# A decoder trunk on one core: router by token tile, top-2 by comparing all pairs, and the setup of the experts in another order

## The reference, cut to what matters

```python
def moe_swiglu(x, router, w13, w2):
    logits = (x @ router).astype(jnp.float32)             # 256 x 8
    top_vals, top_idx = lax.top_k(logits, TOP_K)          # TOP_K = 2
    top_w = jax.nn.softmax(top_vals, axis=-1)
    gates = jnp.einsum('bsk,bske->bse', top_w, jax.nn.one_hot(top_idx, N_EXPERTS, dtype=jnp.float32))
    out = jnp.zeros_like(x)
    for e in range(N_EXPERTS):                            # 8 experts, width 3584
        out = out + gates[..., e:e + 1].astype(x.dtype) * swiglu(x, w13[e], w2[e])
    return out
```

## Time and profile before

| | us |
|---|---|
| median of 3 runs | 1828.35 |
| lowest, highest | 1824.98, 1829.74 |
| the profiled execution | 1832.96 |
| its span, first to last instruction | 1831.1 |
| mean granted clock of TensorE, share of full | 0.98 |
| busy: PE, DVE, ACT | 1743.0 (95%), 1291.2 (71%), 983.5 (54%) |

### The profile page before, as it was taken

The page is one execution under the profiler, slowest core; times in us unless marked ns, Lnnn a source line. Parts: engine busy times, 40 slices in busy tenths (PEclk is TensorE's granted clock), DMA queues, the critical chain, the costliest instruction groups (busy, mean ns, idle before and its releaser), DMA issues.

```text
span 1831.1 us, 21349 instructions
## 1 busy us (share of the span) xinstructions
PE 1743.0 (95%) x7850; PEld 1354.0 (74%) x7850; DVE 1291.2 (71%) x1209; ACT 983.5 (54%) x871; POOL 22.1 (1%) x32
## 2 busy tenths in 40 slices
PE   7989998998989999879999999999999999999996
PEld 6846565887777465657888888888888888888884
DVE  4465525554454655248989889899899898898996
ACT  4353222434333422117767777677777776777772
POOL 0001000000000010000000000000000000000000
PEclk9999999999999999979999999999999999999998
DMA  8512432645634233278999999999999999999991
GB/s 290 183 63 83 154 116 96 225 150 177 217 138 146 93 115 108 76 253 297 358 344 368 371 346 362 353 358 366 338 363 370 347 359 359 349 369 343 364 369 43
DMA packets 206470, 465.94 MB, mean 254 GB/s; under 512 B 11952, under 2 KB 14544, under 8 KB 206416
## 3 DMA queue, kind: packets, MB, share of 16 engines
q1 hardware_dynamic: 200880, 463.76, 70.4%
q10 hardware_dynamic: 5536, 1.45, 0.3%
HBM read 464.13 MB, written 1.05 MB: 254 GB/s over the span
## 4 chain that ended last, share of the span: by engine, by line
PE 90%; DVE 5%; ACT 2%; DMA 1%; issue 1%; ACTq 0%; DVEq 0%; SPq 0%
PE ps L1483 22%; PE ps L1927 16%; PE ps L1929 16%; PE ps L1928 16%; PE ps L1513 5%; PE ps L1849 3%; PE ps L1907 2%; PE ps L1916 1%; DVE w_lo L903 1%; PE ps L1444 1%; PE ps L1639 1%; PE ps L1775 1%; PE ps L1757 1%; PE ps L1694 1%; PE ps L1596 1%
## 5 line engine op out<-in xcount | busy, mean ns | idle before, releaser
L903 DVE TENSOR_TENSOR w_lo<-ring,w_hi 128x2048 fp32r<-128x2048 f32 x336 | 768.0, 2290 | 120.4 <-ACT w_hi L586 117.6
L586 ACT CAST w_hi<-ring 128x2048 fp32r<-128x2048 f32 x336 | 642.0, 1911 | 279.9 <-PE ps L1929 265.0
L1927 PE MATMUL ps<-w_hi,xe_hi 128*128 128x512 f32 x896 | 353.2, 394 | 3.2 <-DVE w_lo L903 1.8
L1929 PE MATMUL ps<-w_hi,xe_lo 128*128 128x512 f32 x896 | 349.3, 390 | 0.0
L1928 PE MATMUL ps<-w_lo,xe_hi 128*128 128x512 f32 x896 | 348.7, 389 | 0.0
L1927 PEld LDWEIGHTS ps<-w_hi,xe_hi 128*128 128x128 f32 x896 | 168.3, 188 | 38.7 <-DVE w_lo L903 2.8
L1929 PEld LDWEIGHTS ps<-w_hi,xe_lo 128*128 128x128 f32 x896 | 168.2, 188 | 35.7
L1928 PEld LDWEIGHTS ps<-w_lo,xe_hi 128*128 128x128 f32 x896 | 168.4, 188 | 33.8
L1927 PE MATMUL ps<-w_hi,he_hi 128*128 128x512 f32 x448 | 178.2, 398 | 0.0
L1929 PE MATMUL ps<-w_hi,he_lo 128*128 128x512 f32 x448 | 174.8, 390 | 0.0
L1928 PE MATMUL ps<-w_lo,he_hi 128*128 128x512 f32 x448 | 174.4, 389 | 0.0
(11 more groups left out here) (264 smaller groups left out, 1778.4 us busy)
## 6 DMA issues: line engine op xcount, KB each, us to landing
ring<-in_moe_w_dram SPq DMA_DIRECT2D x336, 1024.0 KB, 5.2
ring<-in_ffd_w_dram SPq DMA_DIRECT2D x31, 1024.0 KB, 5.1
ring<-in_w_in_dram SPq DMA_DIRECT2D x24, 1024.0 KB, 5.2
ring<-in_xa_wkv_dram SPq DMA_DIRECT2D x16, 1024.0 KB, 5.0
ring<-in_w_out_dram SPq DMA_DIRECT2D x8, 1024.0 KB, 5.0
ring<-in_xa_wq_dram SPq DMA_DIRECT2D x8, 1024.0 KB, 5.0
ring<-in_xa_wo_dram SPq DMA_DIRECT2D x8, 1024.0 KB, 5.0
ring<-in_ffd_w_dram SPq DMA_DIRECT2D x4, 512.0 KB, 3.5
```

The source lines that it names most:

```text
L586: act.copy(w_hi[:, q % SPLIT_SLOTS, :], ring[:, q % RAW_SLOTS, :]).then_inc(hi_ready, 1)
L903: dve.tensor_tensor(w_lo[:, q % SPLIT_SLOTS, :], ring[:, q % RAW_SLOTS, :], w_hi[:, q % SPLIT_SLOTS, :].bitcast(F32), ALU.subtract).then_i ...
L1927: pe.matmul(ps[:, bank, :], x_hi, hi[:, c, cols], start=first, stop=False)
L1929: return pe.matmul(ps[:, bank, :], x_lo, hi[:, c, cols], start=False, stop=last)
```

## The change

- TensorE turns tile 0 of the last `x2` between the two output panels of tile 1, multiplies tile 0's router products behind the second panel, and tile 1's behind its own transposes. ACT copies tile 0's blocks ahead of its first three casts. VectorE copies tile 0's blocks ahead of the first residual, moves low half 0 between the two residuals, and low half 1 between the last layer norm and the copy of tile 1.
- The two largest are found by comparing all pairs: `order` of an expert is the number of experts that stand above it (a greater logit, or an equal one of a lower index), and `chosen` is `order < 2`. The one-hot rows `oh` and the two logits come after `chosen_ready`.
- `slot` is (rank + 1) * chosen, one step, and is compared with a row 1..128 (`place`).
- The two count products go behind the gathers, into bank 4, with a semaphore of their own; the accumulator's setup goes behind the second `xe_lo`.
- `item(0)` waits for the first half of the gather before its first weight half and for the second before its second.

```diff
--- before.py
+++ after.py
@@ -108,10 +108,11 @@
         lower = (i // half) % 2 == 0
         level[:, v, :] = (block[:, None] == block[~lower][None, :]) & lower[:, None]
     square = np.stack([np.eye(P), i[:, None] < i[None, :], np.ones((P, P)),
-                       np.broadcast_to(i[None, :], (P, P))], 1).astype(np.float32)
+                       np.broadcast_to(i[None, :] + 1, (P, P))], 1).astype(np.float32)
     freq = (THETA ** (-np.arange(0, 2 * ROPE, 2, dtype=np.float32) / np.float32(2 * ROPE))).astype(np.float32)
     e = np.arange(NE, dtype=np.float32)
-    rows = np.concatenate([freq, NE - e, e, np.arange(EXTRA, dtype=np.float32)])
+    earlier = (e[None, :] < e[:, None]).astype(np.float32).ravel()
+    rows = np.concatenate([freq, e, earlier])
     rows = np.broadcast_to(rows[None, :], (P, rows.size)).astype(np.float32)
     return {"mask_a": mask_a, "mask_b": mask_b, "level": level, "square": square,
             "rows": np.ascontiguousarray(rows)}
@@ -136,11 +137,11 @@
         x = sb("x", [P, T, D])
         ln_gb = sb("ln_gb", [P, 2, D])
         square = sb("square", [P, 4, P])
-        ident, before, ones, iota = (square[:, n, :] for n in range(4))
-        rows = sb("rows", [P, ROPE + 2 * NE + EXTRA])
+        ident, before, ones, place = (square[:, n, :] for n in range(4))
+        rows = sb("rows", [P, ROPE + NE + NE * NE])
         freq = rows[:, 0:ROPE]
-        desc = rows[:, ROPE:ROPE + NE]
-        eid = rows[:, ROPE + NE:ROPE + 2 * NE]
+        eid = rows[:, ROPE:ROPE + NE]
+        earlier = rows[:, ROPE + NE:].rearrange("p (e f) -> p e f", e=NE)
         w_router = sb("w_router", [P, KC, NE])
         stats = sb("stats", [P, T, 2, 6])
         mv = sb("mv", [P, T, 2])
@@ -149,6 +150,8 @@
         mhalf = sb("mhalf", [P, 8])
 
         lg = sb("lg", [P, 2, T, NE])
+        above = sb("above", [P, 2, T, NE, NE])
+        order = sb("order", [P, T, NE])
         oh = sb("oh", [P, 2, T, NE])
         rtmp = sb("rtmp", [P, T, NE])
         rmx = sb("rmx", [P, 4, T])
@@ -299,7 +302,8 @@
         hT_psum = [sem(f"hT_psum{t}") for t in range(T)]
         hT_sb = [sem(f"hT_sb{t}") for t in range(T)]
         w2_ready = sem("w2_ready")
-        logit_psum, chosen_ready, rank2_psum = sem("logit_psum"), sem("chosen_ready"), sem("rank2_psum")
+        logit_psum, chosen_ready = sem("logit_psum"), sem("chosen_ready")
+        rank2_psum, count_psum = sem("rank2_psum"), sem("count_psum")
         gate_diff, gate_exp = sem("gate_diff"), sem("gate_exp")
         table_ready = sem("table_ready")
         raw_in = [sem(f"raw_in{s}") for s in range(RAW_SLOTS)]
@@ -727,10 +731,11 @@
                     turn_split(TURN["x2", l], (0,))
                     split_high(2)
                 else:
+                    turn(TURN["x2", l], xT, (0,))
                     act.wait_ge(xo_ready, T * (l + 1))
                     for q in range(SPLIT_SLOTS):
                         high(q, 0, first=True)
-                    turn(TURN["x2", l], xT)
+                    turn(TURN["x2", l], xT, (1,))
                 if l == 0:
                     for n in range(FFN_CHUNKS + 1):
                         if n < FFN_CHUNKS:
@@ -1224,10 +1229,12 @@
                 if l == 0:
                     split_low(1)
                 else:
-                    low(0, 0)
+                    turn(TURN["x2", l], xT, (0,))
                 residual(l, o_p, 0, 1)
                 if l == 0:
                     split_low(1)
+                else:
+                    low(0, 0)
                 residual(l, o_p, 1, 1)
                 if l == 0:
                     turn_split(TURN["x2", l], (0,))
@@ -1235,8 +1242,8 @@
                     layer_norm(3 * l + 1, x, 1)
                     turn_split(TURN["x2", l], (1,))
                 else:
-                    turn(TURN["x2", l], xT, (0,))
                     layer_norm(3 * l + 1, x, 1)
+                    low(1, 0)
                     turn(TURN["x2", l], xT, (1,))
                 if l == 0:
                     for n in range(FFN_CHUNKS + 1):
@@ -1280,45 +1287,43 @@
                     turn_split(TURN["x3", l], (0,))
                     split_low(3)
 
-            low(1, 0)
             low(2, 0)
 
-            dve.wait_ge(logit_psum, 1)
-            dve.tensor_scalar(acc, x[:, :, :], ALPHA, None, ALU.mult).then_inc(acc_init, 1)
             full = [P, T, NE]
 
             def over(v):
                 return v.unsqueeze(2).to_broadcast(full)
 
+            pairs = [P, T, NE, NE]
+            dve.wait_ge(logit_psum, T)
             done(dve.tensor_copy(lg[:, 0], ps[:, 4, 0:T * NE].rearrange("p (t e) -> p t e", t=T)))
+            done(dve.tensor_tensor(above[:, 0], lg[:, 0].unsqueeze(2).to_broadcast(pairs),
+                                   lg[:, 0].unsqueeze(3).to_broadcast(pairs), ALU.subtract))
+            done(dve.scalar_tensor_tensor(above[:, 1], above[:, 0], 0.0, earlier.unsqueeze(1).to_broadcast(pairs),
+                                          ALU.is_equal, ALU.mult))
+            done(dve.scalar_tensor_tensor(above[:, 0], above[:, 0], 0.0, above[:, 1], ALU.is_gt, ALU.add))
+            done(dve.tensor_reduce(order[:, :, :], above[:, 0], AX, ALU.add))
+            done(dve.tensor_scalar(chosen[:, :, :], order[:, :, :], 2.0, None, ALU.is_lt))
+            dve.sem_inc(chosen_ready, 1)
+            dve.memset(slot[:, :, :], -1.0)
             for c in range(2):
-                done(dve.tensor_reduce(rmx[:, c, :], lg[:, c], AX, ALU.max))
-                done(dve.tensor_tensor(rtmp[:, :, :], lg[:, c], over(rmx[:, c, :]), ALU.is_equal))
-                done(dve.tensor_tensor(rtmp[:, :, :], rtmp[:, :, :], desc.unsqueeze(1).to_broadcast(full), ALU.mult))
-                done(dve.tensor_reduce(rmx[:, 3, :], rtmp[:, :, :], AX, ALU.max))
-                done(dve.tensor_tensor(oh[:, c], rtmp[:, :, :], over(rmx[:, 3, :]), ALU.is_equal))
-                if c == 0:
-                    done(dve.tensor_scalar(rtmp[:, :, :], oh[:, 0], -3e38, None, ALU.mult))
-                    done(dve.tensor_tensor(lg[:, 1], rtmp[:, :, :], lg[:, 0], ALU.add))
-            done(dve.tensor_tensor(chosen[:, :, :], oh[:, 0], oh[:, 1], ALU.add))
-            dve.sem_inc(chosen_ready, 1)
-            done(dve.memset(slot[:, :, :], -1.0))
-
-            dve.wait_ge(rank2_psum, 1)
-            done(dve.tensor_tensor(rtmp[:, :, :], ps[:, 5, 0:T * NE].rearrange("p (t e) -> p t e", t=T), chosen[:, :, :],
-                                   ALU.mult))
-            done(dve.tensor_scalar(lg[:, 0], chosen[:, :, :], -1.0, 1000.0, ALU.add, ALU.mult))
-            done(dve.tensor_tensor(slot[:, :, 0:NE], rtmp[:, :, :], lg[:, 0], ALU.add))
-
-            def select(i):
-
-                for t in range(T):
-                    ins = dve.tensor_scalar(sel[:, t, :], iota, slot[:, t, bass.ds(i, 1)], None, ALU.is_equal)
-                ins.then_inc(sel_ready, 1)
-
-
+                done(dve.tensor_scalar(oh[:, c], order[:, :, :], float(c), None, ALU.is_equal))
+                done(dve.tensor_tensor(lg[:, 1], oh[:, c], lg[:, 0], ALU.mult))
+                done(dve.tensor_reduce(rmx[:, c, :], lg[:, 1], AX, ALU.add))
             done(dve.tensor_tensor(rmx[:, 2, :], rmx[:, 1, :], rmx[:, 0, :], ALU.subtract))
             dve.sem_inc(gate_diff, 1)
+
+            dve.wait_ge(rank2_psum, 1)
+            done(dve.scalar_tensor_tensor(slot[:, :, 0:NE], ps[:, 5, 0:T * NE].rearrange("p (t e) -> p t e", t=T), 1.0,
+                                          chosen[:, :, :], ALU.add, ALU.mult))
+
+            def select(i):
+
+                for t in range(T):
+                    ins = dve.tensor_scalar(sel[:, t, :], place, slot[:, t, bass.ds(i, 1)], None, ALU.is_equal)
+                ins.then_inc(sel_ready, 1)
+
+
             select(0)
             dve.sem_inc(he_ready, 1)
             dve.sem_inc(y_split, 2)
@@ -1335,6 +1340,7 @@
 
             for g in range(2):
                 gather_low(0, -2, g, g + 1)
+            dve.tensor_scalar(acc, x[:, :, :], ALPHA, None, ALU.mult).then_inc(acc_init, 1)
             dve.wait_ge(gate_exp, 1)
             done(dve.tensor_scalar(rmx[:, 3, :], rmx[:, 2, :], 1.0, None, ALU.add))
             done(dve.reciprocal(rmx[:, 0, :], rmx[:, 3, :]))
@@ -1349,7 +1355,8 @@
 
                 if part == 0:
 
-                    done(dve.tensor_scalar(cnt[:, 0, :], ps[:, 5, 32:32 + NE], float(P), None, ALU.is_gt))
+                    dve.wait_ge(count_psum, 1)
+                    done(dve.tensor_scalar(cnt[:, 0, :], ps[:, 4, 32:32 + NE], float(P), None, ALU.is_gt))
                     done(dve.tensor_tensor_scan(cnt[:, 1, :], ones[:, 0:NE], cnt[:, 0, :], 0.0, ALU.mult, ALU.add))
                     done(dve.tensor_scalar(table[:, 0:1], cnt[:, 1, NE - 1:NE], float(NE), None, ALU.add))
                     done(dve.tensor_tensor(cnt[:, 2, :], cnt[:, 1, :], cnt[:, 0, :], ALU.subtract))
@@ -1405,7 +1412,7 @@
                     if q == 20:
                         select(i + 1)
```

(39 more changed lines are left out.)

4 lines of the change are left out of this document (2 added, 2 removed).

## The result

The changed kernel takes 1817.58 us (1813.92 to 1820.27, 6 runs) against 1829.61 us (1824.98 to 1834.03, 6 runs) for the kernel before: ratio 0.9937, 95% interval 0.9919 to 0.9954. Its profiled execution has a span of 1816.1 us and a mean granted clock of 0.988.

The account below looks back on a forecast made before the run. Matmuls pace the experts, so the turn-taking chain before the first expert matmul counts: 3.6 + 1.1 + 1.2 + 0.9 + 0.6 + 1.0 = 8.4 us off the median 1828.35 gives 1820.0 us, range 1815.5 to 1824.6.

Parts of the forecast that it names:

- router of tile 0 into the gap: Before tile 1's transposes: tile 0's router products run in TensorE's 5.39 us idle gap, so logits come 3.6 us earlier.
- accumulator off the path: In front of the logits' copy on VectorE: moving the accumulator's setup behind the second xe_lo saves 1.1 us.
- choice by pairs, to the end of chosen: From logits' copy to chosen: 14 instructions in 2.87 us become a sum of 1.66, saving 1.2 us.
- ranks, to the slots' step: From chosen to the next VectorE step: five rank products become three, 2.52 us becomes 1.65, saving 0.9 us.
- slots, to the gathers: Between the ranks and the gathers: one fused step is left of the first four, saving 0.6 us.
- gathers' end to first expert product: TensorE waits for the first xe_lo alone, count products go in the gap: 1.0 us saved, 0.6 at the other bound.
- The bound: Experts are paced by matmuls, so an earlier first expert matmul, 822.04 us now, is worth its whole lead to the end.
- The pair instructions: In the choice of experts: four instructions on 128 elements take 1.28 to 1.54 us with gaps; 1.28 was taken.
- A: Tile 0's router products hold the clock up before tile 1's transposes: 1.4 us more gain, 1818.6 us; chance 0.12.
- B: Clock comes back later, with gathers, counts and first 12 expert matmuls low: gain 4.7 us, 1823.6 us; chance 0.14.
- C: Experts begin at the low clock and stay there: 1835 us with the first six halves low; chance 0.05.
- D: Tile 0's router misses the gap because its xT copy is late: 3.5 us come back, 1823.4 us; chance 0.05.

Follow-up runs that it names:

- order_undone: Changed kernel with the router's order as before: both tiles turned behind the second panel, router products together, low halves put back; 1825.32 us, ratio 0.998.
- lows_later: Changed kernel with low half 1 behind the copy of tile 1's xT and low half 2 behind the selection; 1820.63 us, one execution.
- pairs_undone: Changed kernel with the two experts chosen by maximum, comparison, tie-break and masking as before; 1813.94 us, one execution.
- both_banks: Changed kernel with the wait for both halves of the gather before the first expert product; 1821.05 us, one execution.
- narrow_fit: Changed kernel with TensorE's gaps filled by 14, 8, 8 and 4 idle products of 8 columns; ratio to before 0.9968.
- warm_lows_values: Changed kernel with low halves 1 and 2 later, 3, 0, 2 and 0 idle products, logit values and ACT's exponential behind the gathers; ratio to before 0.9932.
- The second measurement: The changed kernel measured once more without edit; 1820.94 us against 1829.52 for the kernel before, ratio 0.9959.
- warm_fit: Changed kernel with 3.5, 2, 2 and 1 idle products of 512 columns cut to TensorE's gaps; ratio to before 0.9942.
- warm: Changed kernel with six, three, three and two idle 128x512 products in TensorE's gaps; ratio to before 0.9949.
- warm_fit_values: Changed kernel with 3.5, 2, 2 and 0 idle products of 512 columns, logit values and ACT's exponential behind the gathers; ratio to before 0.9937.

## Why the prediction was right, step by step

The forecast was 8.4 us off the median; the stretch gave 9.63, of which 0.89 is the clock in the gathers, which the prediction named as a spread and didn't price in the sum. The steps, each as the lead gained at it from the traces set together at the panel's start:

```
step                                    predicted   measured   from
router of tile 0 into the gap           3.6         3.66       806.42 - 776.37 against 797.52 - 771.13
accumulator off the path                1.1         1.14       807.56 - 806.42
choice by pairs, to the end of chosen   1.2         1.19       2.87 against 1.68
ranks, to the slots' step               0.9         0.78       2.52 against 1.74
slots, to the gathers                   0.6         0.73       1.48 against 0.75
gathers                                 0           0.89       6.17 against 5.28
gathers' end to first expert product    1.0         1.24       1.44 against 0.20
sum                                     8.4         9.63
```

- **The bound** was read rightly: from the first expert product to the end all profiles have between 1007.98 and 1009.14 us, whatever came before.
- **The router.** Its part is right, and order_undone shows it with the low halves' places (3.70). Inside it two small terms were off. Tile 1's transposes come 0.51 us earlier against the panel and not 0.16: the eight between the panels cost 0.87 us (778.08 to 778.95) and not 1.04, and TensorE answers the norm (790.74) in 0.11 us where it took 0.31, for which no run here shows a cause. When the router starts, 0.25 of the 0.51 is left: the transposes were 0.16 shorter (1.78 against 1.94), but they end at 792.63, low half 1 holds VectorE and the copy starts at 793.10, 0.47 later where it had been 0.04. So the half was not quite hidden, as the prediction had it; lows_later takes 0.41 of the router's wait away.
- **The pair instructions** took 0.29 us each, at the lower of the two bounds; a broadcast operand on both inputs (the row at 797.73) took as long as none (798.38). pairs_undone has 1.03 for it, which is the 1.19 less 0.14 that the values cost behind the new choice.
- **Ranks.** Here the cover was thin, and the prediction's 1.57 us of values against 1.65 of products came out the other way: the difference ends at 800.63 + 0.16 = 800.79, the ranks at 800.18 + 0.57 = 800.75, and the row of the slots' step at 800.94 shows no wait for TensorE. In pairs_undone, without those values, the same step comes 0.14 us sooner behind `chosen` and does wait for TensorE. That is the missing 0.1.
- **Half a gather** is worth 1.24 and not 1.0. The prediction put the count products at 0.43 us behind the gathers; from their start to the first expert product they took 0.36 (806.81 to 807.17), and they start 0.16 before the gathers' end as the profile has it, so 0.20 is left. both_banks shows the wait at 1.25.
- **Rivals.** A, that the router's narrow products hold the clock up: the granted clock was 0.55 on the mean from 790 to 800 us in the changed kernel, and in narrow_fit it fell behind nothing but such products. The Trainium skill, "TensorE: Matmul & The Clock Gate", section "What's actually happening", has the clock follow how busy the engine has been. The trace does not agree with that if busy is what the profile counts: narrow_fit fell at 100% busy. B and C, the clock coming back later: where it had fallen it was back before the gathers ended in all profiles. Counted from the gathers' start it came back sooner than in the kernel before in the changed kernel's two profiles (gathers 5.28 and 5.29) and later in lows_later and warm_lows_values (6.57 and 6.61, against 6.17), and never as late as the experts. D: the router of tile 0 did run in the gap. No run showed the slower side.

The mechanism is right up to the gathers: 7.4 us were forecast there and 7.50 measured. The good fit of the time is in part luck. The median of 1817.58 lies 2.4 below the forecast of 1820.0, but the forecast was taken off a median of 1828.35 that six runs put at 1829.61: the gain was 12.0 us where 8.4 was forecast, 1.2 of the difference by the steps above, 0.89 of that the clock in the gathers, and the rest outside the changed stretch. The second measurement gave 8.6 (1829.52 less 1820.94). The setup of the accumulator was not undone by itself; its 1.14 us are from the two traces alone.

No version here beats the changed kernel by its time. warm_fit has a stretch 3.1 us shorter in its profile, but its ratio to before, 0.9942 (0.9924 to 0.996), can't be told from 0.9937 and 0.9959: 3.1 us are 0.17%, and these intervals are twice as wide.

## What to carry to other kernels

Where four engines take turns and none is full, price the chain step by step from start-to-start times, and put in front of each wait the work that doesn't need it; each microsecond then reaches the end whole if what follows is paced by the engine that starts sooner. When the scatter of a run is as large as the gain, set the two traces together at the last instruction that the change doesn't touch and measure the stretch: here three profiles with the same instructions agreed to 0.01 us up to the gathers, while the starting point moved by 12 us over all profiles. Look at the clock in that stretch too, since it alone moved the gathers by 0.88 us between those three. Work that fills TensorE's gaps for the sake of its clock has to fit the gap (5.40 us in one of 3.19 gave nothing), narrow products did not do here what wide ones did, and the wide ones did not do it in every profile.

## What the runs showed of the hardware that was not expected

- A busy TensorE can lose its clock. With gaps filled by 128x8 products the granted clock went from 1.00 to 0.50 though every slice of 2 us shows 2.00 us busy; with 128x512 products in the first of these gaps it stayed at 1.00 there in all five profiles that had them, and in warm and warm_fit up to the experts. In the other three it fell later, in warm_fit_values with TensorE busy for 2.00 us of both slices from 792 to 796 us.
- The gathers' 32 instructions took 3.73 to 6.61 us in fourteen profiles, by when the clock came back or whether it had fallen, and the same code up to there gave 5.28, 5.29 (the changed kernel) and 6.16 (both_banks).
- With the same code ahead of it, output panel `o_p` of tile 1 started anywhere from 765.51 to 777.50 us, later in the profiles with more time at the low clock ahead of it.
